# Sixteen rows of one matrix per layer split into small transfers of three rows

## What is computed

```python
for i in range(2):
    h = rms_norm(x, norm_mix_g[i])
    x = x + (pool_mixer(h) if i == 0 else diff_attention(h))
    h = rms_norm(x, norm_ffn_g[i])
    x = x + hier_moe(h)          # 32 experts, each token to two of one group
return rms_norm(x, final_g)
# one expert: (silu(xb @ w1[e]) * (xb @ w3[e])) @ w2[e]
```

## Time and profile before

| | |
|---|---|
| median of three runs | 1078.57 us |
| the profiled execution | 1080.94 us |
| its span in the profile | 1078.8 us |
| TensorE busy | 857.8 us, 80% of the span |
| VectorE busy | 363.4 us, 34% |
| ScalarE busy | 227.8 us, 21% |
| DMA, mean over the span | 395 GB/s |
| DMA in most of the 40 slices | 424 to 429 GB/s |

### The profile page before, as it was taken

One profiled execution on the slowest core, in us unless ns is written; L12 is line 12 of the kernel. 1 busy time (PEld: TensorE's weight loads), 2 busy tenths in 40 slices (PEclk: granted clock), 3 DMA queues, 4 the chain that ended last, 5 costly groups with the idle time before them and its releaser, 6 DMA issues.

```text
span 1078.8 us, 18543 instructions
## 1 busy us (share of the span) xinstructions
PE 857.8 (80%) x8092; PEld 500.7 (46%) x8092; DVE 363.4 (34%) x866; ACT 227.8 (21%) x549; POOL 0.2 (0%) x4
## 2 busy tenths in 40 slices
PE   8897767778676867789999998889958677767784
PEld 6743433344333434444788464544434343434442
DVE  4642222323222322226466464233323222232223
ACT  3421111111111111113143333112111111111112
POOL 0000000000000000000000000000000000000000
PEclk9898989979889988999999999999989888998998
DMA  9999999999999999999911989999999999999994
GB/s 370 424 426 429 426 428 426 427 428 428 426 427 426 426 428 426 428 415 408 413 44 54 424 308 376 427 426 427 426 426 427 428 427 426 428 426 428 428 420 184
DMA packets 37902, 425.98 MB, mean 395 GB/s; under 512 B 3762, under 2 KB 4914, under 8 KB 12724
## 3 DMA queue, kind: packets, MB, share of 16 engines
q1 hardware_dynamic: 37812, 424.68, 93.8%
HBM read 423.62 MB, written 1.05 MB: 394 GB/s over the span
## 4 chain that ended last, share of the span: by engine, by line
PE 43%; DMA 39%; DVE 11%; ACT 3%; issue 2%; SPq 1%; ACTq 0%; DVEq 0%
DMA store<-in_moe_w 39%; PE ps L619 14%; PE ps L683 8%; PE ps L928 5%; PE ps L763 5%; DVE store L1414 3%; PE ps L982 2%; DVE hT L1472 2%; DVE store L1422 1%; ACT store L1106 1%; PE ps L503 1%; PE ps L566 1%; DVE store L1416 1%; DVE store L1418 1%; PE ps L889 1%
## 5 line engine op out<-in xcount | busy, mean ns | idle before, releaser
L619 PE MATMUL ps<-store 128*32 128x256 f32 x4224 | 286.1, 430 | 138.2 <-DMA store<-in_moe_w 127.0
L619 PEld LDWEIGHTS ps<-store 128*32 128x32 f32 x4224 | 162.4, 123 | 271.5 <-issue 214.5
L1412 DVE TENSOR_SCALAR store<-store 128x128 f32<-128x128 f32 (+1 forms) x64 | 14.7, 229 | 471.9 <-ACT store L1106 471.9
L683 PE MATMUL ps<-store 128*32 128x256 f32 x2032 | 122.5, 382 | 33.4 <-DVE store L1422 32.8
L1106 ACT ACTIVATE store<-ps 128x256 f32<-128x256 f32 x64 | 24.5, 383 | 498.2 <-PE ps L619 498.1
L546 PE MATMUL ps<-store,h_sb 128*128 128x256 f32 x512 | 127.6, 392 | 0.0
L1472 DVE COPY hT<-ps 32x512 f32<-32x512 f32 x112 | 76.5, 683 | 123.5 <-PE ps L683 122.7
L546 PEld LDWEIGHTS ps<-store,h_sb 128*128 128x128 f32 x512 | 92.0, 189 | 36.3 <-issue 26.3
L683 PEld LDWEIGHTS ps<-store 128*32 128x32 f32 x2032 | 59.7, 109 | 92.4 <-DVE store L1422 56.9
L1118 ACT COPY hT<-ps 32x512 f32<-32x512 f32 x112 | 64.7, 578 | 114.4 <-PE ps L683 113.7
L1079 ACT ACTIVATE store<-ps,cst 128x256 f32<-128x256 f32 (+1 forms) x144 | 58.3, 459 | 102.2 <-PE ps L546 95.9
(11 more groups left out here) (193 smaller groups left out, 489.8 us busy)
## 6 DMA issues: line engine op xcount, KB each, us to landing
store<-in_moe_w SPq DMA_DIRECT2D x177, 2048.0 KB, 31.9
store<-in_moe_w SPq DMA_DIRECT2D x15, 1024.0 KB, 11.8
store<-in_moe_w SPq DMA_DIRECT2D x18, 512.0 KB, 25.7
store<-in_attn_wv SPq DMA_DIRECT2D x2, 2048.0 KB, 23.1
store<-in_attn_wq SPq DMA_DIRECT2D x2, 2048.0 KB, 21.5
store<-in_attn_wk SPq DMA_DIRECT2D x2, 2048.0 KB, 25.9
store<-in_attn_wo SPq DMA_DIRECT2D x2, 2048.0 KB, 23.6
spare<-in_moe_w SPq DMA_DIRECT2D x1, 2048.0 KB, 23.6
```

What stands on the lines that cost most here:

```text
L619: mm = pe.matmul(gu_ps[SB * j:SB * (j + 1), b, :, :], xg[:, u, kt, b, k, :], gate_and_up(kt)[:, :, P * j:P * (j + 1)], start=(kt == 0 and ...
L683: mm = pe.matmul(y_ps[SB * i:SB * (i + 1), b, :], actT[:, b, SB * j:SB * (j + 1)], wj[:, 256 * i:256 * (i + 1)], start=(j == 0 and b == 0) ...
```

## The change

In layer 0 the chunk 60 (`w1` of expert 20) and in layer 1 the chunk 72 (`w1` of expert 24) are no longer one transfer of 128 rows. Rows whose number leaves 0 to 5 when divided by 8 go in six transfers of 16 rows, eight apart. Rows that leave 6 or 7 go in ten transfers of three rows, 40 partitions apart, and the last two such rows (126 and 127) in a transfer of one row each. That is 18 transfers in place of one; every row goes to the same place in the ring as before. Two new semaphores count them: `s_most` the six, `s_few` the ten and the first single row; the slot's own semaphore is raised by the last single row. TensorE waits for all three before it reads the chunk.

```diff
+        s_most, s_few = sem("s_most"), sem("s_few")
+        UNEVEN = ((0, 60), (1, 72))
                     sp.wait_ge(used[j], it * BODY + (layer * NE + e + 1))
+                    if (layer, c) in UNEVEN:
+                        src = chunk_parts(layer, c // CPE, c % CPE)
+                        for r in range(6):
+                            sp.dma_start(ring[r:P:8, c % RING, :], src[r:P:8, :]).then_inc(s_most, 16)
+                        for r in (6, 7):
+                            for g in range(5):
+                                three = slice(8 * g + r, 8 * g + r + 81, 40)
+                                sp.dma_start(ring[three, c % RING, :], src[three, :]).then_inc(s_few, 16)
+                        for r in (6, 7):
+                            sp.dma_start(ring[120 + r:121 + r, c % RING, :], src[120 + r:121 + r, :])                              .then_inc(loaded[c % RING] if r == 7 else s_few, 16)
+                        return
                     load(c % RING, chunk_parts(layer, it * BODY + c // CPE, c % CPE), loaded[c % RING])
...
                         pe.wait_ge(loaded[c % RING], (u0 + c // RING + 1 - ahead) * 16)
...
+                        if (layer, c) in UNEVEN:
+                            pe.wait_ge(s_most, 16 * 6 * (layer + 1))
+                            pe.wait_ge(s_few, 16 * 11 * (layer + 1))
                         return c % RING
```

## The result

The changed kernel takes 1098.99 us (median of four runs, 1097.27 to 1099.75) against 1078.72 us for the kernel before on the same chip; the ratio is 1.0192, 95% interval 1.018 to 1.0205. It is some 20 us slower, where 1.6 us less was forecast, and it lies outside the range of 1076.1 to 1088.0. The profiled execution took 1099.75 us with a span of 1097.6 us. In each of the two matrices 32 rows go in the small transfers (ten of three rows, two of one), not sixteen as the title has it.

A forecast was written before the change was run, and what follows sets the result against it. The weight stream bounds the kernel, through the DMA engine that finishes last. Gains of 0.45 us in layer 0 and 1.15 in layer 1 make 1.6 us less: 1079.3 profiled, 1077.0 us as median; range 1076.1 to 1088.

The forecast's parts named there:

- The bound: Through the later two thirds of either layer's experts, the weight stream sets the pace at 426 GB/s, not the arithmetic.
- The six transfers of 16 rows put one row on each engine, as before: In chunks 60 and 72, these transfers move no load between engines; a row costs 0.615 us.
- The term set to zero: For the transfers of 16 rows in chunks 60 and 72, no cost was counted beyond 0.615 us a row.
- an outermost dimension under 16: Rule against the change: it confines a transfer to that many engines; by it 12.3 us more in all.
- The gain from moving rows: At the ends of both layers' streams, 13 engines lose two rows each: 0.45 us and 1.15 us less, 1.6 in sum.
- The end of layer 1: Sign of being right: DMA share falls later and faster there, first and last engine some 7 us apart or less.
- the likeliest case: Receivers of the moved rows are among the seven engines that finish early: 1076.1 to 1079.8 us, chance 0.54.
- More issues: On SyncE, 18 issues instead of one cost 5.6 to 21 us per chunk, hidden by queued work; taken as nothing.
- TensorE's waits: Two more waits before each chunk's first use cost nothing unless it is late; then up to 6 us once.
- late receivers: Rival at both stream ends: engines receiving rows are among the nine late ones; 1083 to 1091 us, about 1087, chance 0.33.
- rows that don't move: Rival: three-row transfers keep the engines of their partitions, so only issues are added; 1078.6 us, chance 0.08.
- a standing SyncE: Rival: small transfers fill the receivers' queue and stall SyncE, 2 to 6 us per layer; 1082 to 1091 us, chance 0.05.

## Why the prediction was wrong

**The bound: right, and it is why the change hurts.** The stream sets the pace, and 21.4 us taken from it came out as 18.8 us of span.

**"The six transfers of 16 rows put one row on each engine, as before": here it failed.** The count of rows per engine was right, the conclusion that this costs nothing was not. As before they are in number, not in place: a row's engine in a transfer of 16 rows eight apart is mostly not the engine at home there. The run of such transfers alone lost as much time as the change (ratios 1.0177 and 1.0192), so did the 64-row halves (1.0184), and rows at home lost nothing beyond their bytes. The sum took 0.615 us a row as a property of the engine; it held only while each engine wrote its own eight partitions, as in every chunk before (the halves and quarters of the last expert are cut by columns and keep all 128 partitions). With guests it was 1.18 us, for the guests, for their hosts and, from two guests at two homes on, for every engine. The term set to zero measured 9.6 us per layer: 1097.26 - 1078.12 = 19.1 us for two chunks in the run of transfers of 16 rows alone.

The rule that bears on this stands in another page than the one that the prediction weighed: the Trainium skill's "SBUF — State Buffer", section "Door 1: The DMA port swizzle (why `[64,N]` ≈ `[32,N]`)", states that partitions 0 to 63 reach only half of the 16 ports and gets 196 GB/s there; the two transfers of 64 rows agree with 237 GB/s. An estimate from the port map of the Trainium skill gives the destination seven partitions apart 14 or 15 ports and so nearly full speed; it ran at 224 GB/s, and the measurement decides. The rule of the Trainium skill that was weighed, an outermost dimension under 16, speaks of the number of engines; that was not what cost, since three rows at home on three engines left 424 GB/s.

**The gain from moving rows: not to be had this way.** Redistribution alone, by columns, made the kernel 0.83% slower. The moved rows are guests by construction: the receivers write into the homes of the engines that are to be relieved, three at a time, and that alone gave 244 GB/s where the sum had priced nothing but their bytes. The end of layer 1 after does look as the prediction asked, as the earlier trace rows for the kernel after:

```profile
1078.00:1079.00 1.00, 1.00 (x20) 0.41 (x16) 0.00 (x0) 0.00 (x0) 0.00 (x0) 1.00 1.02 401
1080.00:1081.00 1.00, 0.42 (x8) 0.34 (x12) 0.00 (x0) 0.00 (x0) 0.00 (x0) 1.00 0.79 328
1082.00:1083.00 1.00, 1.00 (x7) 0.87 (x6) 0.84 (x2) 0.09 (x1) 0.00 (x0) 1.00 0.54 221
1084.00:1085.00 1.00, 0.52 (x12) 0.35 (x16) 0.40 (x1) 0.93 (x3) 0.00 (x0) 1.00 0.31 127
1086.00:1087.00 1.00, 0.41 (x8) 0.02 (x1) 0.52 (x2) 0.00 (x0) 0.00 (x0) 1.00 0.01 4
```

From the end of the last full microsecond, 1079, to 1086 it is some 7 us where it was 9 (1057 to 1066), and more engines run longer (0.79 where 0.60 stood). That fits rows that went to early engines, as the likeliest case had it, though no view names engines. Layer 0 does not look so, as the earlier trace rows for the kernel after:

```profile
546.00:548.00 2.00, 2.00 (x12) 1.49 (x10) 1.79 (x5) 0.00 (x0) 0.00 (x0) 1.00 0.88 369
548.00:550.00 2.00, 2.00 (x11) 1.77 (x10) 0.64 (x3) 1.33 (x7) 0.00 (x0) 1.00 0.78 328
```

The next stretches of 2 us have shares of 0.73, 0.42 and 0.06. More engines run longer here too, but from first to last it is some 8 us, not under the 7.0 of before. A gain that these views would price at 1 to 2 us is nothing beside the 21 us spent on the way. What share of the 21.4 - 18.8 us it gave back was not separated: the kernel of transfers of 16 rows alone, which redistributes nothing, has the same span of 1097.6 us, with 17.2 us missing by the same sum over slices in place of 21.4.

**More issues: right.** 12.0 and 11.5 us of SyncE in the two layers, between the 5.6 and 21 of the prediction, and no dip in the DMA share. **TensorE's waits:** up to 6 us was allowed for, 8.50 us came, because the chunk was late for another reason. **The rivals:** late receivers would have kept 426 GB/s throughout; rows that don't move would have left the time; a standing SyncE would have shown a share below 1.0. None of these signs was seen. All three priced where a row is done or when it is issued, none how long a row takes, so the range could not hold the result.

## What to carry to other kernels

Count for each transfer not only how many rows an engine gets, but whether it writes them where it writes in the ordinary 128-row transfers that run beside it; a matrix cut by partitions (16 eight apart, 64 of 128, three 40 apart) lost that, and cost itself and its neighbours half of the speed. Cut by columns over all 128 partitions instead, as the kernel before does for its last expert (397 GB/s at a share of 1.01 near its end), or send few rows to the homes of the engines that carry them. This was seen with transfers that run beside a full stream; how they fare alone was not run. And when a share of DMA near 1.0 comes with half of the GB/s, ask how long a row takes before asking who is idle.

## What the runs showed that was not expected

One engine writing at another's home cost a sixteenth of the bandwidth (397 of 426 GB/s); two, at two homes, cost half of it on all 16 engines (224 GB/s), and sixteen cost no more (224 to 228 GB/s), unless they crowd into few homes (172). The Trainium skill, in "DMA: Bandwidth & Descriptors", section "Back-pressure in remote DMA", tells for transfers between cores that a saturated port clogs the way back to the engines that share the path. The 224 GB/s of two guests would fit such a mechanism inside one core, but no run here shows the path itself.

Moving a row to an engine that will be idle later was priced at its bytes. Neither form tried here, by partitions or by columns, cost so little: a row handed to an engine outside its home slowed down the very engine that it was to relieve.
